# A hybrid layer with 32 experts: weights of the last two experts in pieces, a mask by replacement, pages given up sooner, and 20 experts in a loop on TensorE

## The reference

```python
logits = xf @ w_router + b_router                  # 256 x 32
top_vals, top_idx = lax.top_k(logits, 4)
gates = softmax(top_vals)
# for each expert e, on the rows xb of the tokens that chose it:
hgl = xb @ w1[e] + b1[e]                           # 1024 -> 2048
glu = minimum(hgl[:, :1024], 7.0)
lin = clip(hgl[:, 1024:], -7.0, 7.0)
act = glu * sigmoid(1.702 * glu) * (lin + 1.0)
y = act @ w2[e] + b2[e]                            # 1024 -> 1024, times the gate, added to the token
```

## Time and profile before

| | us (records: a count) |
|---|---|
| median of three runs | 1365.48 |
| the profiled execution | 1365.87 |
| its span | 1364.1 |
| TensorE busy | 1308.2 (96%) |
| TensorE weight loads busy | 730.0 (54%) |
| TensorE matmul records and weight load records | 7410 and 7410 |
| VectorE busy | 427.0 (31%) |
| ScalarE busy | 361.4 (26%) |
| moved by DMA | 471.84 MB, mean 346 GB/s |

### The profile page before, as it was taken

How to read it: one execution, slowest core, us unless ns; L and a number is a source line. 1 busy time by engine, 2 the same in 40 slices (tenths; PEclk the granted TensorE clock), 3 DMA queues, 4 the chain that set the end, 5 groups by cost and what they waited for, 6 DMA issues and landing times.

```text
span 1364.1 us, 17321 instructions
## 1 busy us (share of the span) xinstructions
PE 1308.2 (96%) x7410; PEld 730.0 (54%) x7410; DVE 427.0 (31%) x806; ACT 361.4 (26%) x558; POOL 44.7 (3%) x65
## 2 busy tenths in 40 slices
PE   7999999999999999999999999999899999899997
PEld 6999999999999433333333333333333333333332
DVE  5775767576553311211211111111112111112111
ACT  4855455654433211111111111111111111111102
POOL 3001310001001000000000000000000000000000
PEclk8999999999999999999999999999999999999999
DMA  7545454479848999999999999999999999999994
GB/s 224 157 131 158 146 155 124 131 213 332 287 149 312 388 423 428 417 431 430 430 430 432 431 434 432 430 429 430 430 431 431 429 431 432 435 433 429 431 427 182
DMA packets 87179, 471.84 MB, mean 346 GB/s; under 512 B 7194, under 2 KB 68770, under 8 KB 70212
## 3 DMA queue, kind: packets, MB, share of 16 engines
q1 hardware_dynamic: 86880, 470.71, 85.5%
q10 hardware_dynamic: 228, 0.07, 0.0%
HBM read 469.72 MB, written 1.05 MB: 345 GB/s over the span
## 4 chain that ended last, share of the span: by engine, by line
PE 72%; DMA 25%; DVE 1%; ACT 1%; issue 0%; ACTq 0%; DVEq 0%
DMA arena<-in_w_expert_in 22%; PE ps L972 19%; PE ps L1017 12%; PE ps L629 7%; PE ps L630 7%; PE ps L631 7%; PE ps L940 3%; PE ps L925 3%; DMA arena<-in_w_expert_out 3%; PE ps L620 1%; PE ps L622 1%; PE ps L621 1%; PE ps L932 1%; PE ps L948 1%; PE ps L997 1%; PE ps L991 1%
## 5 line engine op out<-in xcount | busy, mean ns | idle before, releaser
L972 PE MATMUL ps<-arena 128*64 128x512 f32 x2048 | 460.7, 605 | 33.2 <-DMA arena<-in_w_expert_in 32.7
L972 PEld LDWEIGHTS ps<-arena 128*64 128x64 f32 x2048 | 148.9, 139 | 338.4 <-issue 289.2
L1788 DVE TENSOR_SCALAR arena<-ps 128x512 f32<-128x512 f32 x32 | 22.1, 692 | 672.3 <-PE ps L972 672.3
L1017 PE MATMUL ps<-arena 128*64 128x512 f32 x1024 | 226.8, 595 | 1.3 <-DMA arena<-in_w_expert_out 0.9
L629 PE MATMUL ps<-A_hi,w_hi 128*128 128x256 f32 x576 | 167.8, 291 | 5.5 <-DVE A_lo L1411 4.2
L630 PE MATMUL ps<-A_lo,w_hi 128*128 128x256 f32 x576 | 164.9, 286 | 0.0
L631 PE MATMUL ps<-A_hi,w_lo 128*128 128x256 f32 x576 | 164.8, 286 | 0.0
L1446 DVE TENSOR_TENSOR w_lo<-w_raw,w_hi 128x1024 fp32r<-128x1024 f32 x118 | 142.0, 1245 | 63.0 <-ACT w_hi L1123 62.9
L1017 PEld LDWEIGHTS ps<-arena 128*64 128x64 f32 x1024 | 71.0, 137 | 137.4 <-issue 136.7
L1347 ACT ACTIVATE arena<-arena 128x512 f32<-128x512 f32 x32 | 20.2, 630 | 448.3 <-DVE arena L1788 448.3
L1123 ACT ACTIVATE w_hi<-w_raw 128x1024 fp32r<-128x1024 f32 x120 | 119.8, 1047 | 27.6 <-DMA w_raw<-in_w_out 7.2
(11 more groups left out here) (300 smaller groups left out, 1335.0 us busy)
## 6 DMA issues: line engine op xcount, KB each, us to landing
arena<-in_w_expert_in SPq DMA_DIRECT2D x50, 4096.0 KB, 38.5
arena<-in_w_expert_out SPq DMA_DIRECT2D x24, 4096.0 KB, 40.0
arena<-in_w_expert_in SPq DMA_DIRECT2D x20, 2048.0 KB, 15.4
w_raw<-in_w_in SPq DMA_DIRECT2D x32, 1024.0 KB, 5.5
arena<-in_w_expert_out SPq DMA_DIRECT2D x11, 2048.0 KB, 15.6
arena<-in_w_expert_in SPq DMA_DIRECT2D x16, 1024.0 KB, 10.4
arena<-in_w_expert_out SPq DMA_DIRECT2D x10, 1024.0 KB, 10.1
w_raw<-in_w_cross_kv SPq DMA_DIRECT2D x8, 1024.0 KB, 7.4
```

Of the source, the lines that this page charges most:

```text
L972: last = mm(ps[64 * half:64 * (half + 1), b, :], xg_cols[:, 2 * h + c, s, :], columns[:, :, half, :], start=False, stop=(s + h + c == 3), ...
L1017: last = mm(ps[64 * half:64 * (half + 1), 3, :], at_cols[:, c, h, :], w[:, at:at + 512], start=(h + c == 0), stop=(h + c == 4))
L1788: V_.tensor_scalar(glu, ps[:, 0, :], LIMIT, None, ALU.min).then_inc(glu_ready, 1)
```

## The change

1. The waits and the order of the last pieces on SP: 9,0 goes out right after 3,1; 6,0 waits for the lower parts of the last unit but one only, 5,0 for the projection of the last unit but one; 9,1 keeps its place.
2. Both w2 chunks of the last two experts (n = 94 and 95) come in four pieces of 1 MB, each with its own semaphore. `last_two` takes them piece by piece: two pieces of expert 30, the activations of 31, two more pieces of 30, one piece of 31, then scatter and gates, then the other three. The activations of 31 go to `xgT` and its result to PSUM bank 2, so that neither waits for the buffers of 30.
3. The mask: the places 4 to 7 of the sorted eight are set to a number that no logit has, the four largest are replaced in a copy of the logits (`match_replace`), and the mask is where copy and logits differ. Index lookup, conversion, comparison and sum go.
4. TensorE does experts 7 to 26 in a loop of four rounds of five (`pe.Fori`); the bias matmuls of the experts' outputs (b2) move from ahead of expert 16 to ahead of the loop.

```diff
+            piece(9, 0)
+            for k in range(2):
+                piece(8, k)
+            sp_.wait_ge(w_lo_ready, 2 * (NU - 1))
+            piece(6, 0)
             sp_.wait_ge(w_lo_ready, 2 * NU)
+            piece(6, 1)
+            sp_.wait_ge(w_done, 2 * (NU - 1))
+            piece(5, 0)
             sp_.wait_ge(w_done, 2 * NU)
+            piece(5, 1)
+            for k in range(2):
+                piece(7, k)
             sp_.wait_ge(ms_psum, 2)
+            piece(9, 1)
...
+                    if n >= PIECES:
                         for k in range(2):
                             cols = slice(PAGE * k, PAGE * (k + 1))
+                            sp_.dma_start(e_half(n, h)[:, cols], e_source(n, h)[:, cols]).then_inc(last_loaded[n - PIECES][2 * h + k], 16)
...
+                pe.wait_ge(at_ready, i + 1)
+                for k in range(2):
+                    out_piece(0, at_cols, 3, k)
                 acts(i + 1)
+                out_piece(0, at_cols, 3, 2)
+                out_piece(0, at_cols, 3, 3).then_inc(y_psum, 1)
+                pe.wait_ge(at_ready, i + 2)
+                out_piece(1, xg_cols, 2, 0)
                 scattered(i + 1)
                 gates(i + 1)
+                for k in range(1, 4):
+                    last = out_piece(1, xg_cols, 2, k)
+                last.then_inc(y_psum, 1)
...
+            with pe.Fori(first, first + 4) as group:
+                for k in range(5):
+                    item(5 * group + (looped - 5 * first + k), five_parts(group, first, looped + k))
+            for i in range(looped + 20, NE - 2):
                 expert(i)
...
+            dve.wait_ge(top_ready, 1)
+            link(V_.memset(v8[:, :, TOPK:8], NO_LOGIT))
             for tb in range(TB):
-                last = V_.max_index(i8[:, tb, :], v8[:, tb, :], lg[:, tb, :])
+                last = V_.match_replace(taken[:, tb, :], v8[:, tb, :], lg[:, tb, :], NO_LOGIT)
             link(last)
-            link(V_.tensor_copy(i8f[:, :, :], i8[:, :, :]))
-            for tb in range(TB):
-                last = V_.tensor_tensor(chosen[:, tb, :, :], iota[:, 0, 0:NE].unsqueeze(1).to_broadcast([P, TOPK, NE]),
-                                        i8f[:, tb, 0:TOPK].unsqueeze(2).to_broadcast([P, TOPK, NE]), ALU.is_equal)
-            link(last)
-            for tb in range(TB):
-                last = V_.tensor_reduce(msk[:, tb, :], chosen[:, tb, :, :].rearrange("p k e -> p e k"), AX.X, ALU.add)
+            last = V_.tensor_tensor(msk[:, :, :], taken[:, :, :], lg[:, :, :], ALU.not_equal)
             last.then_inc(msk_ready, 1)
```

More of the change, by code:

```diff
@@ L34 @@
 BY_HALF = 21
-LAST = CHUNKS * NE - 1
+LAST_TWO = CHUNKS * (NE - 2)
+PIECES = CHUNKS * NE - 2
 EPS = 1e-6
@@ L39 @@
 MASKED = -1e30
+NO_LOGIT = -3e38
 FOX_SCALE = 128 ** -0.5
@@ L231, in layer_program @@
         pe2, pb2 = table(1, NE), table(1, NE)
+        taken = by_block(chosen_at[:, 0:64])
         v8, i8f = (tiles(ap, TB) for ap in (lambda t: (t[:, 0:16], t[:, 16:32]))(table(1)))
@@ L297, in layer_program @@
         e_loaded = [sem(f"e_loaded{b}") for b in range(len(W_AT))]
-        last_loaded = [sem(f"last_loaded{k}") for k in range(4)]
+        last_loaded = [[sem(f"last_loaded{b}_{k}") for k in range(4)] for b in range(2)]
         e_used = sem("e_used")
@@ L344, in by_half @@
         def by_half(n):
[L345 removed]
+            return n < BY_HALF or n >= LAST_TWO
         filled, loads = [0] * 11, {}
@@ L350, in layer_program @@
                 b_ = e_slot(n_, h_) - (0 if by_half(n_) else h_)
-                if h_ == 0 or by_half(n_):
+                if n_ < PIECES and (h_ == 0 or by_half(n_)):
                     filled[b_] += 32 if 2 * n_ + h_ < 11 else 16
@@ L1012, in weights_out, with out_pass @@
                     for c in range(4):
[L1013 to L1018, removed]
-                    last.then_inc((e_used, y_psum)[h], 1)
+                        last = out_pass(at_cols, 3, w, h, c)
+                    last.then_inc((e_used, y_psum)[h], 1)
+            def out_pass(cols, bank, w, h, c):
+                for half in range(2):
+                    at = D * c + 512 * half
+                    last = mm(ps[64 * half:64 * (half + 1), bank, :], cols[:, c, h, :], w[:, at:at + 512],
+                              start=(h + c == 0), stop=(h + c == 4))
+                return last
             def item(i, parts):
@@ L1033, in last_two, with out_piece @@
             def last_two(i):
-                first, second = parts_of(i), parts_of(i + 1)
-                weights_in(i, first)
+                def out_piece(b, cols, bank, k):
+                    pe.wait_ge(last_loaded[b][k], 16)
+                    for c in (2 * (k % 2), 2 * (k % 2) + 1):
+                        last = out_pass(cols, bank, e_half(PIECES + b, k // 2), k // 2, c)
+                    return last
+                weights_in(i, parts_of(i))
                 scattered(i)
@@ L1059, in parts_of @@
                     for h in range(2):
-                        own = n != LAST and (h == 0 or by_half(n))
+                        own = n < PIECES and (h == 0 or by_half(n))
                         out.append((e_half(n, h), loads[n, h] if own else None))
@@ L1065, in expert, with five_parts @@
                 item(i, parts_of(i))
-            for i in range(NE // 2):
+            def five_parts(group, first, i):
+                out = []
+                for h_, (w, loaded) in enumerate(parts_of(i)):
+                    if loaded:
+                        loaded = loaded[0], 48 * group + (loaded[1] - 48 * first)
+                    out.append((w, loaded))
+                return out
+            looped = BY_HALF // CHUNKS
+            first = looped // 5
+            for i in range(looped):
                 expert(i)
@@ L1078, in _ @@
             with pe.If(n_items > NE):
+                pe.wait_ge(y_ready, NE + 1)
                 gather(NE + 1)
@@ L1351, in gates, with acts, result @@
                 A(sgT, ps[:, 3, 0:S], ACT.Copy).then_inc(sgt_ready, 1)
-            def acts(i):
+            def acts(i, to=actT):
                 act.wait_ge(at_psum, i + 1)
-                A(actT, ps[:, 0, :], ACT.Copy).then_inc(at_ready, 1)
-            def result(i):
+                A(to, ps[:, 0, :], ACT.Copy).then_inc(at_ready, 1)
+            def result(i, bank=3):
                 act.wait_ge(y_psum, i + 1)
-                A(ys, ps[:, 3, :], ACT.Copy).then_inc(y_ready, 1)
+                A(ys, ps[:, bank, :], ACT.Copy).then_inc(y_ready, 1)
             def item(i):
@@ L1374, in _ @@
             sigmoid(NE - 1)
+            acts(NE - 1, xgT)
             result(NE - 2)
-            acts(NE - 1)
             gates(NE - 1)
-            result(NE - 1)
+            result(NE - 1, 2)
             with act.If(n_items > NE):
```

20 lines of the change are left out of this document (3 added, 17 removed).

## The result

The changed kernel takes 1356.02 us (median of 4 runs, 1354.95 to 1358.51); the kernel before, on the same chip, 1365.44 us. The ratio is 0.9935, with the 95% interval 0.9922 to 0.9948: 9.4 us less. Forecast were 3.6 us less (1361.9) and a range down to 1359.2. The direction and each mechanism named were there; two sizes were not, and one edit was overlooked.

What follows compares the result with a forecast made beforehand. The prediction took the unbroken weight transfers, plus TensorE's work after the last wait, as the bound. Its terms, 0 + 0.6 + 1.5 + 1.5 = 3.6 us, took 1365.48 to 1361.9 us, range 1359.2 to 1364.5.

Steps and rivals of the forecast that it cites:

- Part 1: Pages on SP given up sooner: the 4.9 us lead returns as a pause before 454, so gain nothing.
- Part 3: Mask by replacement: DVE's chain takes about 1.05 us instead of 1.74; TensorE gains 0.6 us, range 0.3 to 0.6.
- Part 4: Loop on TensorE: register waits cost nothing, fewer instruction fetches save 1.5 us, range 0 to 3.0.
- fetches: Looped code on TensorE stays in place, 15 experts fetch none: 1.0 us by share, 3.0 by period excess; 1.5 taken.
- case A: The forecast itself: loop saves fetches, clock falls at the last wait as before; 1361.9 us, chance 0.40.
- rival C: TensorE's loop code is loaded again each round, saving no fetch: 1363.4 us, 1361.7 without the clock's fall; chance 0.26.
- rival E: Loop cost d per expert makes TensorE the bound, from d = 2.65 us on; 1383 at d = 3.65; chance 0.07.
- 53 us: TensorE's slack before w1 of expert 30: reachable at 1254.5, held by transfers to 1307.62; 2.65 us per looped expert.
- Part 2: Last w2 pieces and new order: three TensorE gaps at the end go, 1.5 us, range 1.0 to 1.6.
- that wait is at 1307.62: TensorE's last wait that counts, for the second half of w1 of expert 30; the end follows from it.
- the gaps in it are 0.87, 0.20, 0.47: TensorE idle between w1 and w2 ends of expert 31 (18.56 us): about 1.5 us, all to go.
- case B: Same as the forecast but without the clock's fall (1.7 us) at the last wait: 1360.2 us, chance 0.20.

Runs made afterwards that it cites:

- e4: Kernel before with only the reordering on SP (pages given up sooner): 1365.67 us, ratio 1.0003.
- e3: Kernel before with only the new mask by replacement: 1364.77 us, ratio 1.0001.
- e1: Kernel before with only the loop (experts 7 to 26 in four rounds of five): 1362.94 us, ratio 0.9982.
- e15: Changed kernel with 128 empty instructions on POOL after a wait for each of 30 experts: 1371.94 us.
- e6: Changed kernel with two loop rounds of ten experts in place of four of five: 1360.85 us, ratio 0.9963.
- e10: Kernel before with w2 of experts 30 and 31 in pieces and the new order, w1 of both whole: 1363.78 us, ratio 0.9989.
- e7: Changed kernel with w1 of experts 30 and 31 in whole chunks, w2 of both in pieces: 1359.26 us, ratio 0.9951.
- e17: Changed kernel itself, run again as control beside the run without the scatter of zeros: 1355.35 us.
- e9: Kernel before with w1 of experts 30 and 31 in halves, w2 of both in pieces and the new order: 1360.15 us, ratio 0.9963.
- e2: Kernel before with only w1 of experts 30 and 31 in halves, w2 as before: 1368.31 us, ratio 1.0022.
- e14: Changed kernel without item 0's zero scatter and with the first page of two expert 0 slots given back 1.76 us earlier: 1355.10 us.
- e12: Changed kernel without the eight scatter records of item 0, which add zeros: 1355.99 us.
- e11: Changed kernel with 8192 empty instructions on POOL: 1392.23 us.

## Why the prediction was wrong

**Part 1 (nothing)** held: e4 took 0.3 us more, not told from none.

**Part 3 (0.6)** held in the profile with 0.76. DVE's chain took 0.84 us (442.13 to 442.97) where I had 1.05. And I took the modelled end of the spare matmuls (443.64) as the earliest start of the matmul behind them. In the changed kernel that matmul starts at 443.16, and their modelled end is 443.32: it is no bound. The times alone can't show it (e3).

**Part 4 (1.5, range 0 to 3.0)** was mis-sized: the term "fetches" is 2.9 us between the two instants, 2.4 us in the times of e1. Both observations were there: the share (1.0) and the excess of the mean period over the quickest (29.34 against 29.14). I took less than the middle, and the second was right: with 45 packets the period is 29.15 on average. A share of all engines is the wrong measure for a transfer that is complete only when its slowest engine is (e15: 430 GB/s as ever, and 17 us lost). That the code is kept, case A, is shown by the packets and by e6; rival C is out. The looped experts that don't wait start 26.58 us apart (from 669.53 to 775.84, over the back edge), so d = 0 and rival E is out. Its 53 us were 50.5, since expert 0 takes 29.12 us and not 26.58 (450.11 to 479.23 before); nothing hangs on that.

**Part 2 (1.5)** is where it failed. The step "that wait is at 1307.62" took the wait for w1 of expert 30 as still there after the change, and "the gaps in it are 0.87, 0.20, 0.47" counted only what lies behind w1 of expert 31. As far as it goes that count was right: e10 has 1.6, and from the end of w1 of 31 to the end of its w2 it is 17.3 us in the changed kernel (1328.02 to 1345.31) where 17.1 was forecast. What it left out is in the diff: `by_half` now holds for all n from 90 on. The description of the change ahead of the prediction leaves it out too. These chunks come in halves with a semaphore each, and the first half of a chunk lands half a chunk (an estimate: 9.73 / 2 = 4.9 us) before the whole. So expert 30 doesn't wait any more (2.35 us), and the fall of the clock that followed the wait in the kernel before (1.7 us) is gone with it: 1.6 + 2.35 + 1.7 = 5.6, measured 5.5. The rests of four kernels show the same three steps: 85.6 before; 84.0 with the pieces of w2 (e10, fall at 30); 82.4 with the pieces and no fall at 30 (e7); 80.1 with w1 in halves too. So case B had the clock's size right, but I gave it as a matter of chance. In part it still is one: the edit moves the last wait to expert 29, where some runs have the fall (e17, e9: rest 81.5) and some have none.

Could it be that w1 in halves is good by itself? No: alone it is slower (e2). TensorE then reaches w2 of expert 30 before the whole chunk is there. In the kernel before, two bounds lay close together: the wait for w1 of 30 with its fall, and the landing of w2 of 30, where only 0.87 us of wait was left. Without the fall TensorE waits 2.67 us there (e3) and gains nothing. Only both edits free both.

**Still open:** why the first freed slot lies between 451.2 and 455.1 us in kernels whose dense stage is the same, or nearly (with the new mask 451.2 to 453.9, without it 452.7 to 455.1; the mask's own 0.76 us is part of that), so that the 1.2 us of the start aren't shown to be the change's; which engines serve which queue, and so why a fetch of POOL costs 0.56 us and one of TensorE 0.2; and why giving back by page (e14) loses what e12 gained.

## What to carry to other kernels

Where all engines of DMA are busy for the whole of a stage, small transfers that nobody counts, code above all, cost by how far they put back the one engine they hit and not by bytes, and the mean rate doesn't show it: look at the DMA share in the last microseconds of the stream; put code that repeats into a loop whose body the engine can keep, and check the count of instruction packets. At the end of a stream of weights, list every wait of the last items with what stands behind it: cutting one transfer finer pays only when the next wait in the chain is cut too. And read a changed condition (`n == LAST` to `n >= LAST_TWO`) for every value that it now takes in.

## What the runs showed of the hardware that I had not expected

- An 8 KB fetch by POOL cost the weights' stream 0.56 us, though by bytes it is 0.02 us of the 16 engines' time (8.2 KB at 430 GB/s); a 16.4 KB fetch by TensorE 0.2 us. At the end of the weights the DMA share was 0.07 for 14 us (e15) and for 20 us (e11), which is one engine of 16.
- The body of five experts (5 x 248 matmul and weight load records, and their waits) was kept by TensorE over four rounds, with no packet on its queue for 457 us; that of ten was fetched again with a stall of 2.96 us.
- With an even period the clock falls at every second wait for long stretches: a wait of 2.35 us is followed by 32 records in 8.78 us, the next wait is then only 0.66 us and followed by 7.09. In the changed kernel it goes so from 866 to 1041 us without a break. But at 1099.52 a wait of 2.35 us is followed by 7.09, and the pattern goes on shifted by one. What the last wait gets depends on such breaks, and differs between runs of one kernel.
- A fall needs no wait: at 641.21 us of the changed kernel, right behind eight small bias matmuls and without idle time, 64 records took 15.65 us instead of 13.90, at a granted clock of 0.88 from 641.2 to 655.2.
